# One decoder layer pair on one core: attention copies in another order, one wait per query tile, and four output-projection units among the last heads

## What is computed

```python
def nsa_mixer(h, ...):
    q, kc, vc, ks, vs, kw, vw, gates = _split(h @ w_in, ...)
    q = rms_norm(q.reshape(bsz, seq, G, HG, DH), q_norm)     # 4 groups x 4 heads of 128
    ...                                                      # k_cmp, v_cmp: 15 compressed keys
    p_c = masked_softmax(q . k_cmp * scale, ...)             # compressed branch
    p_s = masked_softmax(q . k_sel * scale, ...)             # selected branch (all 4 blocks here)
    p_w = masked_softmax(q . k_win * scale, ...)             # window branch (all 256 positions here)
    o = g0 * p_c . v_cmp + g1 * p_s . v_sel + g2 * p_w . v_win
    return o.reshape(bsz, seq, 2048) @ w_out
x = x + nsa_mixer(rms_norm(x, mix_norm[1]), ...)
x = x + conv_ffn(rms_norm(x, ffn_norm[1]), ...)
```

## Times and profile before

| | us |
|---|---|
| median of 3 runs | 2659.84 |
| lowest and highest run | 2658.85, 2662.68 |
| profiled execution, whole | 2655.95 |
| its span | 2654.3 |
| PE busy in the span | 2620.2 (99%) |
| DVE, ACT, POOL busy | 1799.1 (68%), 1426.6 (54%), 220.8 (8%) |

### The profile page before, as it was taken

How to read it: one execution, slowest core, us unless ns; L and a number is a source line. 1 busy time by engine, 2 the same in 40 slices (tenths; PEclk the granted TensorE clock), 3 DMA queues, 4 the chain that set the end, 5 groups by cost and what they waited for, 6 DMA issues and landing times. The chain is left out here.

```text
span 2654.3 us, 46566 instructions
## 1 busy us (share of the span) xinstructions
PE 2620.2 (99%) x15363; PEld 2288.2 (86%) x15363; DVE 1799.1 (68%) x2612; ACT 1426.6 (54%) x2210; POOL 220.8 (8%) x195
## 2 busy tenths in 40 slices
PE   7999999999999999999999999999999999999999
PEld 6888888888888888888888888888888888888888
DVE  7677777765677777775555765665777777775444
ACT  5676767654455555554444445655555555554443
POOL 0122112222100000000111001001300000000000
PEclk9999999999999999999999999998999999999999
DMA  5655555656555555556666555222555555556665
GB/s 186 211 203 193 197 189 198 197 173 187 180 192 188 189 190 190 190 186 184 189 188 197 184 182 195 94 93 88 190 183 188 186 188 189 190 190 185 188 188 168
DMA packets 135255, 481.96 MB, mean 182 GB/s; under 512 B 15104, under 2 KB 17152, under 8 KB 134160
## 3 DMA queue, kind: packets, MB, share of 16 engines
q1 hardware_dynamic: 132480, 467.72, 54.9%
q0 software_dynamic: 2336, 12.65, 1.4%
q10 hardware_dynamic: 368, 0.65, 0.1%
HBM read 478.80 MB, written 2.16 MB: 181 GB/s over the span
## 5 line engine op out<-in xcount | busy, mean ns | idle before, releaser
L980 DVE TENSOR_TENSOR w_lo<-raw,w_hi 128x1024 fp32r<-128x1024 f32 x900 | 1099.8, 1224 | 695.8 <-ACT w_hi L359 694.8
L692 PE MATMUL ps<-xn,w_hi 128*128 128x512 f32 x4768 | 1509.4, 398 | 11.0 <-DVE xn L1006 9.6
L359 ACT ACTIVATE w_hi<-raw 128x1024 fp32r<-128x1024 f32 x900 | 938.1, 1044 | 867.8 <-PE ps L694 848.1
L694 PEld LDWEIGHTS ps<-xn,w_lo 128*128 128x128 f32 x4768 | 897.3, 188 | 212.3
L694 PE MATMUL ps<-xn,w_lo 128*128 128x256 f32 x4768 | 938.4, 278 | 0.0
L692 PEld LDWEIGHTS ps<-xn,w_hi 128*128 128x128 f32 x4768 | 728.4, 189 | 19.5 <-DVE xn L1006 10.3
L692 PE MATMUL ps<-hid,w_hi 128*128 128x512 f32 x1408 | 446.9, 395 | 0.0
L694 PEld LDWEIGHTS ps<-hid,w_lo 128*128 128x128 f32 x1408 | 264.7, 188 | 57.1
L694 PE MATMUL ps<-hid,w_lo 128*128 128x256 f32 x1408 | 288.0, 279 | 0.0
L692 PEld LDWEIGHTS ps<-hid,w_hi 128*128 128x128 f32 x1408 | 219.6, 189 | 5.4
L692 PE MATMUL ps<-y_ssm,w_hi 128*128 128x512 f32 x512 | 161.6, 397 | 0.0
(11 more groups left out here) (240 smaller groups left out, 1783.2 us busy)
## 6 DMA issues: line engine op xcount, KB each, us to landing
raw<-w_gu SPq DMA_DIRECT2D x352, 512.0 KB, 3.6
raw<-w_ssm_in SPq DMA_DIRECT2D x162, 512.0 KB, 3.6
raw<-w_down SPq DMA_DIRECT2D x128, 448.0 KB, 3.4
raw<-w_nsa_in SPq DMA_DIRECT2D x82, 512.0 KB, 3.6
raw<-w_ssm_out SPq DMA_DIRECT2D x64, 512.0 KB, 4.4
raw<-w_down SPq DMA_DIRECT2D x64, 512.0 KB, 3.6
raw<-w_nsa_out SPq DMA_DIRECT2D x32, 512.0 KB, 3.5
wcum<-cum_scratch POOLq DMA_DIRECT2D x8, 1024.0 KB, 8.0
```

What stands on the lines that cost most here:

```text
L359: act.activation(w_hi[:, slot, 0:n * P], raw[:, slot, 0:n * P], ACT.Copy).then_inc(unit_rounded, 1)
L692: pe.matmul(acc[:, 0:2 * n], w_hi[:, slot, cols], x[:, kb, 0:2 * n], start=(kb == 0), stop=False)
L694: mm = pe.matmul(acc[:, n:2 * n], w_lo[:, slot, cols], x[:, kb, 0:n], start=False, stop=(kb == p.blocks - 1))
L980: TT(w_lo[:, slot, 0:n * P], raw[:, slot, 0:n * P], w_hi[:, slot, 0:n * P].bitcast(F32), ALU.subtract).then_inc(unit_split, 1)
```

## The change

Four edits:

- On DVE `pt1_copy` stands ahead of `mask` in a slot, on ACT `pt0_copy` ahead of `exps`, in all groups. Only slot 3 holds both of DVE's, slots 3 and 4 both of ACT's.
- `scores(h)` waits for the first h + 1 query tiles of the group, not for all four.
- `nsa_out` takes four tiles together in its first body: cut 0 of tiles 0 to 3, then cut 1 of tiles 0 to 3. The four cut-0 units (0 to 3) run in group 3 behind slots 0, 1, 4 and 5. Units 2 and 3 use banks 2 and 3, so PE waits ahead of unit 2 for all masks (`masked`). Units 4 to 7 follow behind the attention.
- The rounding and splitting of units 4 to 7 moves from behind the attention into group 3: behind slots 2, 3, 6 and 7.

```diff
--- before.py
+++ after.py
@@ -112,7 +112,7 @@
             ("ssm_out", 32, 16, w_ssm_out, 0, 4, [1, 5, 6, 7], 4),
             ("gu0", 16, 88, w_gu0, 0, 2, None, 2, [3, 4]), ("down0", 44, 16, w_down0, 0, 2),
             ("kvc", 16, 8, w_nsa_in, 1, 2, None, 2, [3, 4]), ("gates", 16, 1, w_nsa_in, 0, 1), ("kvs", 16, 16, w_nsa_in, 9, 2),
-            ("cmp", 32, 4, w_cmp, 0, 4), ("q", 16, 16, w_nsa_in, 25, HPG), ("nsa_out", 16, 16, w_nsa_out, 0, 4, [0, 1, 2, 3], 2),
+            ("cmp", 32, 4, w_cmp, 0, 4), ("q", 16, 16, w_nsa_in, 25, HPG), ("nsa_out", 16, 16, w_nsa_out, 0, 4, [0, 1, 2, 3], 4),
             ("gu1", 16, 88, w_gu1, 0, 2, None, 2, [5, 6]), ("down1", 44, 16, w_down1, 0, 2)):
         last = ph[name] = Phase(last, blocks, tiles, dram, first, per, *more)
     order = list(ph)
@@ -295,6 +295,8 @@
             at = CONST["ffn_norm" if n % 2 else "mix_norm"] + n // 2 * D_TILES
             return cst[:, bass.ds(m + at, 1)]
 
+        EARLY_UNITS, LATE_UNITS = [0, 1, 4, 5], [2, 3, 6, 7]
+
         def is_body(i, n):
 
             return isinstance(i, int) and i == n
@@ -509,7 +511,8 @@
 
                 def body(i, nxt):
                     for v in range(p.body):
-                        round_unit(p.unit0 + RING + v, nxt[v], i, p.body)
+                        if not (p is ph["nsa_out"] and is_body(i, 0) and v < RING):
+                            round_unit(p.unit0 + RING + v, nxt[v], i, p.body)
                         if n < 4 and v == 0 and not is_body(i, 0):
                             weighted(n, i * p.per_body - 1, p)
                         if n < 4 and v - 1 in p.ends(i):
@@ -641,10 +644,10 @@
                     act.wait_ge(exp_done, HPG * G)
                     act.activation(rq[:], ps[6][:, 0:2 * HPG].rearrange("p (c h) -> p c h", c=2), ACT.Sqrt,
                                    bias=eps[:, 1:2]).then_inc(qstd_ready, 1)
+                if 3 <= v <= 6:
+                    pt0_copy(G, v - 3)
                 if 1 <= v <= 4:
                     exps(G, v - 1)
-                if 3 <= v <= 6:
-                    pt0_copy(G, v - 3)
                 if v >= 5:
                     o_round(G, v - 5)
                 if v == 7:
@@ -666,7 +669,13 @@
                         act.activation(krc[:], ps[6][:, P:P + KVG * NCMP], ACT.Sqrt, scale=1.0 / P,
                                        bias=eps[:, 0:1]).then_inc(kstd_ready, 1)
 
-            q_bodies(act, q_body, attend)
+            def last_attend(G, v):
+
+                attend(G, v)
+                if v in LATE_UNITS:
+                    round_unit(ph["nsa_out"].unit0 + RING + LATE_UNITS.index(v), UNIT)
+
+            q_bodies(act, q_body, last_attend)
             out_tiles(ph["nsa_out"], 3)
             ffn(1, ph["gu1"], ph["down1"])
 
@@ -890,7 +899,7 @@
             def scores(G, h):
 
                 pe.wait_ge(masked, G * HPG + h)
-                pe.wait_ge(tile_out, ph["q"].tile0 + HPG + G * HPG)
+                pe.wait_ge(tile_out, ph["q"].tile0 + (h + 1) + G * HPG)
                 for b in range(2):
                     s = ps[2 + b]
                     key0 = (G + (8 + 8 * b)) * T
@@ -955,13 +964,16 @@
             def last_attend(G, v):
 
                 attend(G, v)
-                if v < 2:
+                if v == 0:
                     pe.wait_ge(o_ready, UNIT)
-                    gemm_unit(ph["nsa_out"], 0, v, o_nsa)
+                if v == EARLY_UNITS[2]:
+                    pe.wait_ge(masked, D_TILES)
+                if v in EARLY_UNITS:
+                    gemm_unit(ph["nsa_out"], 0, EARLY_UNITS.index(v), o_nsa)
 
             q_bodies(pe, q_body, last_attend)
             pe.wait_ge(o_ready, D_TILES)
-            for v in range(2, ph["nsa_out"].body):
+            for v in range(RING, ph["nsa_out"].body):
                 gemm_unit(ph["nsa_out"], 0, v, o_nsa)
             gemm(ph["nsa_out"], o_nsa, first=1)
             ffn(1, ph["gu1"], ph["down1"])
@@ -1177,7 +1189,8 @@
 
                 def body(i, nxt):
                     for v in range(p.body):
-                        split_unit(p.unit0 + RING + v, nxt[v], i, p.body)
+                        if not (p is ph["nsa_out"] and is_body(i, 0) and v < RING):
+                            split_unit(p.unit0 + RING + v, nxt[v], i, p.body)
                         if n < 4 and v == 0 and not is_body(i, 0):
                             weighted_rest(n, i * p.per_body - 1)
                         if n < 4 and v - 1 in p.ends(i):
@@ -1362,10 +1375,10 @@
 
             def attend(G, v):
 
+                if 3 <= v <= 6:
+                    pt1_copy(G, v - 3)
                 if v < 4:
                     mask(G, v)
-                if 3 <= v <= 6:
-                    pt1_copy(G, v - 3)
                 if 1 <= v <= 4:
                     normalise(G, v - 1)
                 if v >= 5:
@@ -1404,7 +1417,13 @@
                         dve.memset(prc[:], FLOOR).then_inc(floor_set, 1)
                         dve.wait_ge(floor_set, 1)
 
-            q_bodies(dve, q_body, attend)
+            def last_attend(G, v):
+
+                attend(G, v)
+                if v in LATE_UNITS:
+                    split_unit(ph["nsa_out"].unit0 + RING + LATE_UNITS.index(v), UNIT)
+
+            q_bodies(dve, q_body, last_attend)
             out_tiles(ph["nsa_out"], 3)
             ffn(1, ph["gu1"], ph["down1"])
```

## The result

The changed kernel takes **2644.11 us** (median of 7 runs, 2642.98 to 2645.98); beside it the kernel before took 2658.85 (7 runs, 2651.44 to 2662.68), a ratio of 0.995 with a 95% interval of 0.9936 to 0.9964. The further runs that the experiments brought put the kernel before at a median of 2653.6 and a mean of 2654.6 (105 runs, 2648.2 to 2662.3) and the changed one, with its first seven runs, at a mean of 2644.3 (19 runs, 2642.0 to 2648.8). The means differ by 10.3 us, about 1 us either way: a ratio of 0.996.

What follows compares the result with a forecast made beforehand. TensorE was taken as the bound, busy 2620.2 of 2654.3 us, so only its waits and low clock could be won. Copies 4.46, scores 1.84, group 3's copy 0.37 and clock 2.0 gave 8.7 us: 2651.1 us, range 2646.3 to 2656.7.

Steps and rivals of the forecast that it cites:

- The copies in groups 0 to 2: Attention, slot 4: with DVE's copy ahead of the mask, PE's waits for it go, 4.46 us won.
- the scores: Slot 0 of groups 0 and 3: scores waiting for one query tile win 0.79 and about 1.05, sum 1.84 us.
- Rival 2: DVE late again in slot 5, so the stall moves instead of going: 3.3 us gained, 2656.5; chance 14%.
- There PE has no idle time to fill: Group 3, behind slots 4 and 5: moving units 2 and 3 there is worth 0 by itself.
- the split ahead of the copy: Group 3, slot 2: unit 4's split, 1.14 us, precedes DVE's copy, so 0.37 us is won there, not 1.5.
- The clock: Group 3's second low-clock stretch shortens: 3.2 us at one end, 0 at the other, 2.0 taken.
- At the third I take 0: Low-clock stretch from 1816.9 in group 3, behind the turn: 2.1 us of waiting left, so no clock gain.
- one short fall behind group 3's sums: Group 3: the low-clock stretch behind the query sums should be near 3.4 us, not 9.9.
- the second has the 1.34 of waiting and then the sums: Group 3's 9.9 us low-clock stretch from 1793.2: put behind PE's wait of 1.34 us and then the query sums.
- half of each is lost: Attention's three stretches at 1.2 instead of 2.4 GHz: 1.7, 4.95 and 1.7 us lost.
- Rival 1: Only idle time makes the clock fall, so group 3's second fall goes whole: 11.6 us gained, 2648.2; chance 10%.
- For the median I take off the same 8.7: Whole kernel: the profiled execution's expected gain of 8.7 us, subtracted from the median 2659.84, gives 2651.1.

Runs made afterwards that it cites:

- e1: Kernel before with only the copies of the turned probabilities moved ahead of mask and exps; mean 2650.6 us, 4.6 us less at equal clock.
- e2: Kernel before with only the scores' wait cut from all four query tiles to those needed; mean 2652.6 us, 2.2 us less at equal clock.
- e8: Changed kernel with rounds and splits of units 4 and 5 a slot later, so none stands ahead of the awaited copy; mean 2642.7 us.
- e7: Changed kernel with the scores waiting for all four query tiles again; mean 2649.1 us.
- e9: Changed kernel with the query sums spread between the next full unit's matmuls in all four groups; mean 2646.8 us.
- the fillers: Kernel before with useless matmuls where PE waits in group 3: both places, first scores only, turn of head 1 only; means 2651.5, 2651.5, 2651.9 us.
- e6: Changed kernel without the four units together and the moved rounds and splits; mean 2645.4 us.
- e14: Kernel before with eight useless matmuls ahead of the turn of head 1 in group 3 only; mean 2651.9 us.

## Why the prediction was wrong

**The waits: right in sum.** The sum was 6.67 us; at equal clock the changed kernel is 7.0 us faster, with a standard error of 0.3. The copies in groups 0 to 2 were put at 4.46 and the scores at 1.84; e1 gives 4.6, of which 0.4 (2.43 less 2.0) are group 3's, and e2 2.2. In the profile the turn follows 0.23 us behind the unit, the scores' wait in group 3 is 0.25 ahead of the sums (the sums start 0.61 after the last scores, 1789.52 less 1788.91, where without a wait some 0.36 lie between the two) where 0.35 was expected, and the wait for the copy is 1.92 where 2.0 to 2.2 was. Rival 2, a stall that only moves, was wrong for groups 0 to 2. But in group 3 it is what e1 shows.

**The four units: right sum, wrong account.** "There PE has no idle time to fill" holds for the kernel before, not with the copies ahead: then 0.82 and 0.38 appear, and the units fill them. The prediction weighed each edit against the old timeline instead of against the one that the other edits leave. The 1.1 us of the split ahead of the copy, which it saw, cancels this; e8 takes it back.

**The clock: too small, and its account failed in places.** I took 2.0 us, between 0 and 3.2; the measured part is 3.3. "At the third I take 0" failed: the profile of the changed kernel has no fall behind the turn, though 1.92 us of waiting are left there; e7 and e9, with the same wait, do fall there, so that place goes by chance as well. The forecast of one short fall behind group 3's sums failed too: none of the changed kernel's three profiles has it. The prediction had also misread its own rows: "the second has the 1.34 of waiting and then the sums" puts the sums ahead of a stretch that had begun 2.5 us before them, at 1793.2 against 1795.69. And "half of each is lost" is a little too much: the sums take 3.55 us in such a stretch and 1.93 outside, 0.46 lost of each us, and the line's 2.25 us per 0.001 of 2653 us makes it 0.42. Rival 1, that only idle time makes the clock fall, goes: in groups 0 to 2 it falls behind the sums with none, as the prediction had seen at 1707.6, and so it does behind the key sums at 1605. Just ahead of group 3's long stretch stood the wait of 1.34, with small matmuls on both sides of it.

The Trainium skill ("TensorE: Matmul & The Clock Gate", section "HAM oscillation — how this bites in real kernels") blames idle gaps, in its example waits for DMA that are longer than those here; the fillers agree that idle time counts in group 3 (2.5 to 3.0 us), and the sums point to a second cause. The edits do not add up: together they bring 3.3 us of clock where each alone brings none, and the copies with the tile's wait (e6) already 2.6. That idle time and thin matmuls (sums, turns, outputs) act together in group 3 would explain it but is not shown, nor that the units help the clock; the units with the tile's wait and without the copies were not run. Part of the 3.3 may also come from the place ahead of the attention, which no edit touches. So what made the clock term 3.3 stays open.

**The starting point: wrong, and the step that failed most.** "For the median I take off the same 8.7" took 2659.84, a median of three runs. The kernel before spreads over 14 us with its clock, and its mean over 105 runs is 2654.6, 5.2 lower. From there 8.7 gives 2645.9 and the measured parts (7.0 and 3.3) give 2644.3, the changed kernel's mean. The profiled execution, 2655.95, was the better start, at 2647.3, and lay at hand; the range should have reached down to it less the whole of the clock term. So two terms put the time below the range: the median of three as a start, some 5 us too high, and the clock, 1.3 us too small; the waits account for 0.3.

## What to carry to other kernels

Where a kernel's few runs differ by more than the gain that is looked for, compare at equal granted clock, or take dozens of runs; a median of three is no starting point. Cost several edits in order, each on the timeline that the ones before leave: an edit that has nothing to fill alone may fill what another one opens. A wait of TensorE between stretches of small matmuls can cost more than its length, so put full matmuls there, and put the preparation of the next weights behind the copy that TensorE waits for, not ahead.

## What the runs showed of the hardware

- The 14 us between runs of one kernel on one core follow its mean granted clock, 2.25 us per 0.001 (105 runs).
- Behind a row of sixteen one-column matmuls, 1.9 us, most of them with no idle time of PE ahead, stood a stretch of 3.4 us at 1.2 GHz in 23 of 45 places. With the same matmuls spread between full ones it stood in none of 6.
- Three profiles have a stretch of 10 us at 1.2 GHz that begins right behind a wait of PE of 1.34 us, among thin matmuls; three others with the same wait (e1, e7, e14) have none there.
- Useless matmuls in TensorE's waits made the kernel 3.0 us faster, 1.2 either way (35 runs against 105).
